# Attention stages of a two-block transformer kernel: scan inputs transposed by tile, scores ahead of the turn of probabilities, scan rows split by feature halves, a wait for each operand

## What is computed

```python
s = (jnp.einsum("bqhd,bkhd->bhqk", qn, k_nope)
     + jnp.einsum("bqhd,bkd->bhqk", qp, k_pe)).astype(jnp.float32) * scale
p = jax.nn.softmax(jnp.where(allowed[None, None], s, -jnp.inf), axis=-1).astype(v.dtype)
return jnp.einsum("bhqk,bkhd->bqhd", p, v)
...
return o @ w_o
```

```python
y = ssd_chunked(xs, dt, a, bm, cm, d_skip).reshape(bsz, seqlen, SSD_INNER)
y = rms_norm(y * jax.nn.silu(z.astype(jnp.float32)), ssd_norm).astype(x.dtype)
att = chunked_rel_attention(...).astype(x.dtype)
return jnp.concatenate([y, att], axis=-1) @ w_out
```

## Time and profile before

| | value |
|---|---|
| median of three runs | 1138.82 us |
| the profiled execution: its own time | 1138.02 us |
| its span, first to last instruction | 1136.2 us |
| mean granted TensorE clock | 0.989 of full |
| TensorE busy (matmul) | 1098.6 us, 97% |
| VectorE, ScalarE, GpSimd busy | 694.9, 543.0, 54.7 us (61%, 48%, 5%) |
| weights and data read from memory | 199.95 MB, DMA engines about half busy |
| chain that ended last | 88% TensorE, 7% VectorE, 3% ScalarE |

### The profile page before, as it was taken

One profiled execution on the slowest core, in us unless ns is written; L12 is line 12 of the kernel. 1 busy time (PEld: TensorE's weight loads), 2 busy tenths in 40 slices (PEclk: granted clock), 3 DMA queues, 4 the chain that ended last, 5 costly groups with the idle time before them and its releaser, 6 DMA issues.

```text
span 1136.2 us, 15464 instructions
## 1 busy us (share of the span) xinstructions
PE 1098.6 (97%) x6178; PEld 948.5 (83%) x6178; DVE 694.9 (61%) x778; ACT 543.0 (48%) x631; POOL 54.7 (5%) x103
## 2 busy tenths in 40 slices
PE   8998999999999999999989999999989999999997
PEld 7997888888896788888868888879987777888886
DVE  4666756565765675655676555545966766655552
ACT  4543544443355364444355445435646736444442
POOL 1000000000200000000010000001041011000000
PEclk9999999999999999999989999999989999999999
DMA  9754666654641486555646565545664154655530
GB/s 334 242 184 150 222 194 190 198 193 133 178 161 69 148 263 198 186 185 188 195 136 223 185 194 187 183 140 164 190 189 164 57 186 160 222 191 185 185 111 37
DMA packets 139233, 201.71 MB, mean 178 GB/s; under 512 B 9144, under 2 KB 114848, under 8 KB 139184
## 3 DMA queue, kind: packets, MB, share of 16 engines
q1 hardware_dynamic: 135872, 190.20, 51.9%
q0 software_dynamic: 3312, 10.83, 3.3%
HBM read 199.95 MB, written 1.06 MB: 177 GB/s over the span
## 4 chain that ended last, share of the span: by engine, by line
PE 88%; DVE 7%; ACT 3%; issue 1%; POOL 1%; DMA 0%; SPq 0%; DVEq 0%; POOLq 0%; ACTq 0%
PE up L1580 22%; PE up L1583 11%; PE acc L1591 11%; PE acc L1592 11%; PE acc L1594 11%; PE up L1541 3%; PE up L1542 3%; PE up L1543 3%; DVE weight_lo L1034 2%; PE acc L1703 2%; PE acc L1711 2%; PE acc L1704 2%; PE up L1646 1%; ACT weight_hi L599 1%; PE up L1921 1%
## 5 line engine op out<-in xcount | busy, mean ns | idle before, releaser
L1034 DVE TENSOR_TENSOR weight_lo<-raw,weight_hi 128x2048 fp32r<-128x2048 f32 (+4 forms) x184 | 410.4, 2235 | 147.6 <-ACT weight_hi L599 147.3
L599 ACT ACTIVATE weight_hi<-raw 128x2048 fp32r<-128x2048 f32 (+4 forms) x184 | 342.8, 1869 | 153.0 <-PE acc L1594 137.1
L1580 PE MATMUL up<-x_parts,weight_hi 128*128 128x512 f32 x1088 | 271.4, 391 | 0.0
L1580 PEld LDWEIGHTS up<-x_parts,weight_hi 128*128 128x128 f32 x1088 | 198.7, 188 | 37.6
L1591 PE MATMUL acc<-weight_hi,hh 128*128 128x512 f32 x480 | 189.1, 394 | 5.9 <-DVE hl L1034 5.9
L1592 PE MATMUL acc<-weight_lo,hh 128*128 128x512 f32 x480 | 188.5, 393 | 0.0
L1583 PEld LDWEIGHTS up<-x_parts,weight_lo 128*128 128x128 f32 x1088 | 148.4, 190 | 10.6
L1594 PE MATMUL acc<-weight_hi,hl 128*128 128x512 f32 x480 | 152.4, 392 | 0.0
L1583 PE MATMUL up<-x_parts,weight_lo 128*128 128x256 f32 x1088 | 151.7, 282 | 0.0
L1541 PE MATMUL up<-x_parts,weight_hi 128*128 128x256 f32 x396 | 114.1, 288 | 1.1 <-ACT arena L599 0.6
L1542 PE MATMUL up<-x_parts,weight_hi 128*128 128x256 f32 x396 | 112.4, 284 | 0.0
...
## 6 DMA issues: line engine op xcount, KB each, us to landing
...
```

The costliest lines, as they stand in the source:

```text
L599: return nc.scalar.activation(dst, src, ACT.Copy, **kw)
L1034: return vec.tensor_tensor(dst, whole, high.bitcast(F32), ALU.subtract)
L1580: mm(bank.rearrange("p (a n) -> p a n", a=2), w_h[k], x_parts[:, k, :, :], start=k == 0, stop=k == KD - 1, skip_group_check=True)
```

## The change

Five edits, none of which adds, removes or changes an instruction's work; they move instructions and waits.

1. **UQ.** PE waits for `t_lo` 2 instead of 3 ahead of the first UQ product, and for the third ahead of the second.
2. **Steps.** In both attentions PE issues `scores(g + 2)` ahead of `turn_probs(g)`. In the MLA, `first_rows(1)` moves from step 7 to step 8.
3. **Scan inputs by tile.** PE transposes tile 0 without waiting for `decays`, then does `keys_queries(1)`, then waits for `decays` and transposes tile 1. ACT and DVE take tile 0, the slab of `keys_queries(1)` and tile 1 in that order.
4. **Scan rows by halves.** Normalising, transposing, rounding and splitting y goes first through both tiles of the first half of the features, then through those of the second; PE waits for two low parts ahead of HWO+2 and for four ahead of HWO+4.
5. **`qk_out`.** `scores(0)` of the hybrid attention waits for three copies of queries and keys, `scores(1)` for the fourth.

```diff
--- before.py
+++ after.py
@@ -965,10 +965,14 @@
             act.wait_ge(hy["cum_out"], TILES)
             nc.scalar.activation(dt_work[:, 7, :], acc[:, 2, 32:64], ACT.Exp).then_inc(hy["decays"], 1)
             keys_queries(0)
-            for g in range(4):
-                act.wait_ge(hy["xs_ps"], g + 1)
-                copy(y_tok[:, g // 2, g % 2 * HALF:(g % 2 + 1) * HALF], acc[:, g, :]).then_inc(hy["xs_out"], 1)
+            def rows_out(tile):
+                for h in range(2):
+                    act.wait_ge(hy["xs_ps"], 2 * tile + h + 1)
+                    copy(y_tok[:, tile, h * HALF:(h + 1) * HALF], acc[:, 2 * tile + h, :]).then_inc(hy["xs_out"], 1)
+
+            rows_out(0)
             keys_queries(1)
+            rows_out(1)
             for g in range(SSD_GROUPS):
                 act.wait_ge(hy["cb_ps"], g + 1)
                 copy(cb_off[:, g, :], up[g][:, P:2 * P]).then_inc(hy["cb_act"], 1)
@@ -1006,7 +1010,7 @@
             round_slab(HWO + RING)
             for g in range(4):
                 act.wait_ge(hy["y_ps_t"], g + 1)
-                copy(xh[:, 4 * (g % 2):4 * (g % 2) + 4, (g // 2) * P:(g // 2 + 1) * P],
+                copy(xh[:, 4 * (g // 2):4 * (g // 2) + 4, (g % 2) * P:(g % 2 + 1) * P],
                      up[g][:, :].rearrange("p (k n) -> p k n", k=4)).then_inc(hy["y_hi"], 1)
             for j in (1, 2, 3):
                 round_slab(HWO + j + RING)
@@ -1430,18 +1434,21 @@
             dve.wait_ge(hy["cum_out"], TILES)
             split_slab(HQK + RING)
 
-            for g in range(4):
-                tile, h = g // 2, g % 2
-                dve.wait_ge(hy["xs_out"], g + 1)
-                hd = tile * SSD_HEADS + 8 * h
-                vec.tensor_tensor(heads(xdt[:, tile, h * HALF:(h + 1) * HALF]), heads(acc[:, g, :]),
-                                  per_head(dt[:, hd:hd + 8]), ALU.mult).then_inc(hy["xdt"], 1)
-                if g == 1:
-                    dve.wait_ge(hy["decays"], 1)
-                    dve.wait_ge(hy["xdt"], 2)
-                    vec.tensor_tensor(heads(xdt_end, SSD_HEADS), heads(xdt[:, 0, :], SSD_HEADS),
-                                      per_head(dt_work[:, 7, 0:SSD_HEADS], SSD_HEADS), ALU.mult).then_inc(hy["cb"], 1)
+            def dt_rows(tile):
+                for h in range(2):
+                    g = 2 * tile + h
+                    dve.wait_ge(hy["xs_out"], g + 1)
+                    hd = tile * SSD_HEADS + 8 * h
+                    vec.tensor_tensor(heads(xdt[:, tile, h * HALF:(h + 1) * HALF]), heads(acc[:, g, :]),
+                                      per_head(dt[:, hd:hd + 8]), ALU.mult).then_inc(hy["xdt"], 1)
+
+            dt_rows(0)
+            dve.wait_ge(hy["decays"], 1)
+            dve.wait_ge(hy["xdt"], 2)
+            vec.tensor_tensor(heads(xdt_end, SSD_HEADS), heads(xdt[:, 0, :], SSD_HEADS),
+                              per_head(dt_work[:, 7, 0:SSD_HEADS], SSD_HEADS), ALU.mult).then_inc(hy["cb"], 1)
             split_slab(HQK + 1 + RING)
+            dt_rows(1)
 
             for g in range(SSD_GROUPS):
                 dve.wait_ge(hy["cb_act"], g + 1)
@@ -1501,15 +1508,15 @@
                 vec.tensor_tensor(y, y, z_gate[tile][:, :], ALU.mult).then_inc(hy["y_gated"], 1)
             split_slab(HZ + 2 + RING)
             split_slab(HZ + 3 + RING)
-            for tile in range(TILES):
-                y = y_tok[:, tile, :]
-                dve.wait_ge(hy["rstd"], tile + 1)
-                for c in HALVES:
+            for c in HALVES:
+                for tile in range(TILES):
+                    y = y_tok[:, tile, :]
+                    dve.wait_ge(hy["rstd"], tile + 1)
                     vec.scalar_tensor_tensor(y[:, c], y[:, c], rstd[:, tile:tile + 1], gain2[:, c], ALU.mult, ALU.mult)\
                         .then_inc(hy["y_n"], 1)
             split_slab(HWO + RING)
             for g in range(4):
-                tile, f = g // 2, g % 2
+                tile, f = g % 2, g // 2
                 dve.wait_ge(hy["y_hi"], g + 1)
                 rest(xl[:, 4 * f:4 * f + 4, tile * P:(tile + 1) * P], up[g][:, :].rearrange("p (k n) -> p k n", k=4),
                      xh[:, 4 * f:4 * f + 4, tile * P:(tile + 1) * P]).then_inc(hy["y_lo"], 1)
@@ -1843,9 +1850,11 @@
                     ins = nc.tensor.transpose(up[1 + g][:, n * P:(n + 1) * P], src[:, tile, k * P:(k + 1) * P], ident)
                 ins.then_inc(mla["turned"], 1)
             partner(0)
-            pe.wait_ge(mla["t_lo"], 3)
+            pe.wait_ge(mla["t_lo"], 2)
             for j in range(4):
                 weights(UQ + j)
+                if j == 1:
+                    pe.wait_ge(mla["t_lo"], 3)
                 if j >= 2:
                     pe.wait_ge(mla["q_out"], j - 1)
                 for f in range(2):
@@ -1903,10 +1912,10 @@
 
                 def step(g, between=None):
 
+                    if g + 2 < HEADS:
+                        scores(g + 2)
                     if g < HEADS:
                         turn_probs(g)
-                    if g + 2 < HEADS:
-                        scores(g + 2)
                     if between:
                         between()
                     if g:
@@ -1950,8 +1959,8 @@
             for g in range(HEADS + 1):
                 if g == 1:
                     step(g, values_ready)
-                elif g in (6, 7):
-                    step(g, lambda: first_rows(g - 6))
+                elif g in (6, 8):
+                    step(g, lambda: first_rows((g - 6) // 2))
                 else:
                     step(g)
             last_products(3, CT, [(WO + c, *latent_rows(c), lambda c=c: heads_out(c)) for c in (2, 3)])
@@ -1988,15 +1997,19 @@
 
             keys_queries(0)
 
+            def turn_rows(tile):
+
+                for h in range(2):
+                    for j in range(4):
+                        ins = nc.tensor.transpose(acc[:, 2 * tile + h, j * P:(j + 1) * P],
+                                                  xs_t[:, 4 * h + j, tile * P:(tile + 1) * P], ident)
+                    ins.then_inc(hy["xs_ps"], 1)
+
             pe.wait_ge(hy["xbc"], 4)
+            turn_rows(0)
+            keys_queries(1)
             pe.wait_ge(hy["decays"], 1)
-            for g in range(4):
-                tile, h = g // 2, g % 2
-                for j in range(4):
-                    ins = nc.tensor.transpose(acc[:, g, j * P:(j + 1) * P], xs_t[:, 4 * h + j, tile * P:(tile + 1) * P],
-                                              ident)
-                ins.then_inc(hy["xs_ps"], 1)
-            keys_queries(1)
+            turn_rows(1)
 
             pe.wait_ge(hy["xbc"], 6)
             for g in range(SSD_GROUPS):
@@ -2040,9 +2053,10 @@
                 if p == 0:
                     pe.wait_ge(hy["xdt"], 4)
                     pe.wait_ge(hy["xs_out"], 4)
-                    pe.wait_ge(hy["qk_out"], 4)
+                    pe.wait_ge(hy["qk_out"], 3)
                     pe.wait_ge(hy["off_taken"], SSD_GROUPS)
                     scores(0)
+                    pe.wait_ge(hy["qk_out"], 4)
                     scores(1)
                 else:
                     step(2 * p - 1)
@@ -2060,7 +2074,7 @@
             def turn_y():
 
                 for n in range(2 * TILES):
-                    tile, h = n // 2, n % 2
+                    tile, h = n % 2, n // 2
                     pe.wait_ge(hy["y_n"], n + 1)
                     for j in range(4):
                         f = (4 * h + j) * P
@@ -2083,11 +2097,11 @@
             ins.then_inc(slab_used, 1)
             weights(HWO + 1)
             down_product(HWO + 1, *head_rows(1), CT, between=turn_y)
-            pe.wait_ge(hy["y_lo"], 4)
+            pe.wait_ge(hy["y_lo"], 2)
             for c in range(2):
                 weights(HWO + 2 + c)
                 down_product(HWO + 2 + c, *latent_rows(c), CT)
-            last_products(6, CT, [(HWO + 2 + c, *latent_rows(c), lambda: None) for c in (2, 3)])
+            last_products(6, CT, [(HWO + 2 + c, *latent_rows(c), lambda: pe.wait_ge(hy["y_lo"], 4)) for c in (2, 3)])
             glu_part(1, 7, normed)
```

## The result

The changed kernel takes 1149.28 us (median of four runs, 1148.38 to 1151.73) against 1138.8: 0.9% slower, ratio 1.0094 with a 95% interval of 1.008 to 1.0108. The forecast was 1139.6 with a range of 1135 to 1143.6: it was 9.7 us too low, and the time lies outside the range. The profiled execution is the slowest of the four (1151.73, span 1149.9), so its stages add up to 13.7 us more than those of before, where the medians differ by 10.5. Its mean granted clock is 0.978; that of the other three is 0.981 and 0.982, which comes to 7 to 9 us less at half speed somewhere in the run.

The account below looks back on a forecast made before the run. TensorE was taken as the bound, busy for 97% of the span. Terms -0.5 + 6.6 - 4.9 + 0 + 0.3 - 0.7 = +0.8 us on a median of 1138.82 gave 1139.6 us, range 1135 to 1143.6.

Parts of the forecast that it names:

- UQ: First UQ product: the 0.52 us wait for the latents' low parts goes, -0.5 us; bounds 0 and -0.6.
- Steps of the MLA attention: MLA outputs: five new waits of 1.52 us, less the old 1.02, +6.6 us; bounds +4.1 and +10.6.
- the clock falls in the MLA attention: Rival, MLA steps: one or two stretches of 5 to 7 us at half speed, +3, 1142.6 us; chance 0.14.
- the stretch at 768: Earlier trace: PE idle 1.46 of two us, clock stayed at 1.00; taken as close to the expected 1.52 us waits.
- the stretch at 828: Earlier trace, scan-input transposes after the 4.01 us wait: clock at 0.50; model for the rival's 5 to 7 us stretches.
- The rule of the Trainium skill: Rival, MLA steps: transposes don't count as busy, so four steps run at 1.2 GHz, near 1153 us; chance 0.03.
- Scan inputs: Hybrid entry: 4.01 us wait gone, new 1.4 us wait at the state product, -4.9 us; bounds -6.3 and -2.
- qk_out: Ahead of first scan outputs: scores(0) fills half the 0.9 us wait, ACT and DVE still last; 0 us, at most -0.5.
- Steps of the hybrid attention: Hybrid passes: scores fill odd-step waits of 1.3 us, lost again at even steps; +0.3 us, bounds -1.3 and +0.9.
- Scan rows by halves: Ahead of HWO+2: PE needs two of four low parts, 1.2 us less, DVE stalls 0.5; -0.7 us, bounds -1.3, +0.5.
- the stall of DVE: Scan rows: DVE's second row waits for GpSimd's second root, about half of its 0.93 us, 0.5 us.

Follow-up runs that it names:

- mla_filled: Changed kernel with 12 matmuls of zeros between turn and outputs in MLA steps 2, 3, 4, 5 and 7, filling PE's waits; 1141.81 us.
- mla_back: Changed kernel with only the MLA attention's old step order and first_rows placement put back; 1134.19 us.
- mla_once: Changed kernel with the old step order in both attentions, except the new order in step 2 of the MLA; 1142.17 us, runs at two levels.
- mla_twice: Changed kernel with the old step order in both attentions, except the new order in steps 2 and 4 of the MLA; 1146.49 us.
- mla_once_again: The same kernel as mla_once, run again for another profile; median 1142.07 us, profiled execution 1144.8 us.
- round_first: Changed kernel with the hybrid attention's old order; MLA keeps the new order, but ACT rounds a head's output ahead of its probability copy; 1131.83 us.
- hybrid_late: mla_back with the hybrid attention's old order in steps 0 and 1 and the new order from step 2 on; 1133.55 us.

## Why the prediction was wrong, point by point

- **UQ**, forecast -0.5: -0.72, a little beyond its bound of -0.6.
- **Steps of the MLA attention**, forecast +6.6: the waits cost +6.64 (mla_filled against mla_back), in the five steps named. This mechanism and its size were right. **What failed is the rival "the clock falls in the MLA attention"**, as it was sized: one or two stretches of 5 to 7 us, +3 us, chance 0.14. The low stretch was 27 us long and cost 10.16. The step of the reasoning that failed was that "It decides if four such waits in a row, 4.85 us apart, are too much", with the stretch at 768 of the earlier trace rows as the row that spoke for 1.00. One wait of 1.41 us was enough in both profiles of mla_once, though not the first of mla_twice. And the length after it was taken from the stretch at 828; in the MLA the clock stayed low for 20 us with PE busy throughout (mla_once_again).
- **The rule of the Trainium skill** (TensorE: Matmul & The Clock Gate, Part 4: PE-mode transpose) gave all four steps at 1.2 GHz and "near 1153", chance 0.03; the measured outcome looks like it. That the transposes do it is not shown: no run replaces them, and mla_once_again stays low without any further pause. The transposes alone don't do it: round_first has them in the same places without the waits, and its clock stays at 1.00. The chance of a long low stretch was too small all the same, whatever its cause.
- **Scan inputs**, forecast -4.9: -4.35 at the entry, -4.24 at the scans. The new wait is 2.1 instead of 1.4 us, since the split that the forecast took at 2.29 us took 3.13. The clock stays at 1.00 there in the changed kernel, as forecast; in hybrid_late and mla_once_again (17.29 and 17.26 us to the scans) a low stretch came.
- **`qk_out`**, forecast 0: the 0.9 us wait is gone, the one for `tmp_c` grew by 0.2, and the scans come 0.11 later in relation: 0.
- **Steps of the hybrid attention**, forecast +0.3: +0.98 in passes 2 to 4, just beyond its bound of +0.9. The waits at odd steps were said to be filled by the scores; they are still 1.3 us. On top came 2.46 us of low clock in the first pass, of which the forecast had nothing.
- **Scan rows by halves**, forecast -0.7: -0.64. PE stands idle 0.13 us ahead of the product of the earlier trace rows instead of 1.31. Half of that is given back in a second pause of 0.55 us for y's rows (1.1 us in all, up from 0.6), which is the stall of DVE that the forecast held.

Without the clock the terms sum to -0.72 + 6.64 - 4.24 + 0.98 - 0.64 = +2.0 against a forecast of +0.8, inside the range. The clock added 10.16 + 2.46, and 1.19 came back in column (a), where before has its low stretch of the earlier trace rows at 759 and the changed kernel has none. That is luck: no edit touches this stretch. These are figures of the slowest of the four runs; the medians show 7.5 us for the MLA's clock.
